# Second layer of a two-layer expert network: 64 of 256 tokens gather their rows, the V product is turned round, and VectorE divides in the mixer

## The chip, the cores and the metric

One Trainium2 chip, one of its cores. The metric is the device time in microseconds (us) from launch to end. The engines are PE (TensorE; PEld is its weight loads), DVE (VectorE), ACT (ScalarE), POOL (GpSimd, which issues part of the DMAs) and SP (SyncE, which issues DMAs alone).

## The reference, cut to what matters

256 tokens of width 1024 go through two layers (`first_block`) and a third block (`second_block`, which the change leaves alone). A layer is a mixer (attention and a convolution) and an expert part, `peer`. In layer 0 `peer` also treats 256 context tokens; in layer 1 it treats the 256 tokens alone.

```python
def peer(h, w_pq, sub_keys, u_tab, v_tab):          # h: 256 x 1024 in layer 1
    q = (h @ w_pq).reshape(B, T, PEER_HEADS, 2, PEER_HALF)
    s = jnp.einsum('bthcd,hckd->bthck', q, sub_keys)
    top_s, top_i = lax.top_k(s, PEER_TOPK)
    ...
    expert = i1 * PEER_KEYS + i2                     # 8 heads x 16 = 128 experts of 16384 per token
    w = jax.nn.softmax(best_s, axis=-1)
    ...
        u = jnp.take(u_tab, ec, axis=0)
        act = jax.nn.gelu(jnp.einsum('cd,ced->ce', hc, u), approximate=False)
        v = jnp.take(v_tab, ec, axis=0)
        return jnp.einsum('ce,ced->cd', (act * wc), v)
```

`u_tab` and `v_tab` are 16384 x 1024 in f32, 64 MB each and layer. The mixer's attention is a softmax over 512 keys, 8 heads, then times V.

## The kernel before, in words

**Two ways for a token.** The *dense* way works out gelu(U h) for all 16384 experts and multiplies by a weight that is zero for all but the token's 128. The tables pass once, in 128 tiles a of 128 rows (0.5 MB each), two tiles to a DMA of SP into a ring of four slots. The *gathered* way fetches the 128 chosen rows of U and of V of each token with indirect DMAs of POOL, one token to a partition; VectorE takes each row's product with h (`u_row`) or adds the row times its factor (`v_row`). In layer 0 the first 128 of the 512 tokens are gathered (`b.first` 128), 384 are dense (`b.D`). In layer 1 `b.first` is 0 and all 256 are dense.

**U stage** (`peer` of each engine's program). Each U tile is cut into a high and a low part of type fp32r: ACT casts the high part (`high`, L980), VectorE or POOL subtracts to get the low (`low`, L1415; POOL at L2130). PE multiplies by h in three products over 8 blocks of 128, so 24 multiplies a tile with the tile as the fixed operand and the dense tokens as the moving one (`u_product`, L757). ACT takes gelu (L1229), POOL stores the result to `g_scratch` (L2140).

**The order within it.** The U tiles are the filling between steps of choosing the experts. `early()` gives five steps to a tile, 640 in all, and `FILLS[l]` says how many steps each engine takes after each piece of work: fill_a after each of 4 groups of scores, fill_b after each of 2 groups of candidates (together the *search*, 4 fill_a + 2 fill_b), fill_c three times in the *rest*, and fill_w after each *quad* of 4 tokens whose one-hot rows are built (VectorE L1415 and L1420, ACT L1248 and L1253) and multiplied (L802) to make the weights, which ACT copies out (L1281) and POOL stores (L2170). This goes round per block t of 128 tokens. What is left of the 640 steps then runs by itself: the *tail*. In the search POOL does the low parts of even tiles, in the rest and in the quads VectorE does all. `U_TURNS` names the tiles beside which rows of U are taken; only layer 0 has them.

**V stage.** For each tile a: weigh the gelu by the weights (L1415), split it in high and low, split the V tile, and multiply (L822). The token side `x` is the fixed operand, 128 tokens at a time, the V tile the moving one, 512 columns at a time: 12 multiplies a tile in layer 1, into four PSUM banks. At the end ACT (L1298) and VectorE (L1865) copy the banks out, PE transposes (L534) and VectorE adds to `xT` (`("xp", l, m)`). Rows of V in layer 0 land in 8 buffers, by `V_TURNS`, 128 rows over 118 tiles.

**Mixer.** `attend` takes 16 units in layer 1. VectorE finds the maximum (L1527), ACT takes the exponential with its sum (L1079), VectorE the reciprocal, ACT multiplies the unit by it (L1088), two units behind; then PE transposes it. Between units VectorE does 7 taps of the convolution (L1423).

**Queues that the change touches.** POOL's is in strict order: low parts, gathers (`u_row`, `v_row`: each waits for VectorE to free its buffer), gelu stores, stores of weights, loads of both back (L2180, L2190). SP issues the ring's loads.

Of the kernel before, what the change touches and what calls it, by code (L numbers as in the profile page):

```python
# [60 lines left out]
GATHERED = 128  # L61

U_ROWS, V_ROWS = 4, 8


FILLS = ((6, 10, 14, 3), (12, 22, 20, 2))

ACT_TOKENS = (0, 1)
LAG = 3
# [6 lines left out]
def _u_turns():  # L76
    fill_a, fill_b, fill_c, fill_w = FILLS[0]
    search, rest = 4 * fill_a + 2 * fill_b, 3 * fill_c
    tiles, step = [], search + 2 * fill_c
    for t in range(1, 4):  # L80
        begin, step = step + search, step + search + rest + 32 * fill_w
        tiles += [a for a in range(128) if begin + (10 if t == 1 else 0) <= 5 * a + 3 < (step if t < 3 else 636)]
    turns = [[] for _ in range(128)]
    for i, a in enumerate(tiles):
        turns[a] = list(range(128 * i // len(tiles), 128 * (i + 1) // len(tiles)))
    return turns


U_TURNS = _u_turns()
V_TURNS = [[] for _ in range(6)] + [list(range(128 * i // 118, 128 * (i + 1) // 118)) for i in range(118)] + [[]] * 4  # L90
# [87 lines left out]
class Attention:  # L178
# [3 lines left out]
    def __init__(self, tag, q, kT, vtok, groups, lay, bias=None, sinks=None):  # L182
# [7 lines left out]

        self.score_banks, self.turn_banks, self.out_banks = ((0, 1, 2), (3,), (4, 5)) if bias is None else (
# [19 lines left out]
class Memory:  # L211


    def __init__(self, nc, ctx, A, out, book):
# [10 lines left out]
        self.u_rows = [plain[:, 14336 + 1024 * i:15360 + 1024 * i] for i in range(2)]  # L225
        self.v_rows = [plain[:, 1024 * i:1024 * i + 1024] for i in range(V_ROWS)]
# [36 lines left out]
        self.v_row_in = [signal(f"v_row{i}_in", 16) for i in range(V_ROWS)]  # L263
# [67 lines left out]
    def peer(self, l):  # L331
# [6 lines left out]
        b.first = 0 if l == 1 else GATHERED  # L338
# [3 lines left out]
        b.u_split, b.v_split = ((0, 1, 2, 3),) * 2 if l == 1 else ((0, 1, 4), (0, 1))  # L342
# [4 lines left out]
        if b.first:  # L347
            b.idx = lay.take(128).bitcast(U32)
            b.dot, b.w0 = lay.take(128), lay.take(128)
# [15 lines left out]
        if b.first:  # L365
            b.hx = lay.take(1024)
        b.qT = lay.take(8 * b.T).rearrange("p (t k q) -> p t k q", k=8, q=128)
        if b.first:

            self.u_rows += [b.qT[:, t].rearrange("p k q -> p (k q)") for t in range(2)]  # L370
# [4 lines left out]
        b.sum = lay.take(1024) if b.first else None  # L375
        return b

# [123 lines left out]
def tensor_program(e, M):  # L501
# [125 lines left out]
    def attend(a, side=lambda: None):  # L627
# [10 lines left out]
        def turned(n):  # L638
            N = a.width(n)
            P = a.P3[n % 4][:, 0:N]  # L640
            w.wait_ge(act, ("pn", a.tag, n))
# [91 lines left out]
    def peer(l):  # L733
# [7 lines left out]
        if b.first:  # L741
            for i in range(2):
                w.wait_ge(dve, ("h", ("peer", l), 4 * i + 3))
                o = bank(("hx", i), (act, ("hx", i)))
                transposes(o, [M.ACC[:, 4 * i + k, 0:128] for k in range(4)]).then_inc(pe.after(("hx", i)), 1)
# [33 lines left out]
        for t in range(T // 128):  # L779
# [10 lines left out]
            if 128 * t < b.first:  # L790
                continue
# [4 lines left out]
            for _ in range(32):  # L796
# [14 lines left out]
        for tb in range(D // 128):  # L811
            for half in range(2):
                bank(("y", l, tb, half), (act if half == 0 else dve, ("yout", l, tb, half)), (2 * tb + half,))
        for a in range(128):
            name, x = ("v", l, a), M.AG[(a + 2) % 4]
            v = M.SR[book.buffer.get(name, 0)]
            w.wait_ge(*M.low(name))
            w.wait_ge(dve, ("alow", l, a))
            for tb in range(D // 128):
                for r, c in ((0, 0), (0, 1), (1, 0)):  # L820
                    for half in range(2):
                        ins = e.matmul(M.PS[2 * tb + half][:, :], x[:, r, 128 * tb:128 * tb + 128],  # L822
                                       v[:, c, 512 * half:512 * half + 512], start=(a == 0 and (r, c) == (0, 0)),
                                       stop=(a == 127 and (r, c) == (1, 0)), skip_group_check=True)
                if a == 127:
                    ins.then_inc(pe.after(("y", l, tb), ("used", name), ("vused", l, a)), 1)
# [129 lines left out]
def scalar_program(e, M):  # L956
# [221 lines left out]
    def peer(l):  # L1178
# [26 lines left out]
        def a_high(a):  # L1205
# [5 lines left out]
            elif b.first:  # L1211
                w.wait_ge(pe, ("pu", l, 127))
# [1143 lines left out]
```

## Time and profile before

| | us |
|---|---|
| median of 3 runs | 3453.84 |
| lowest and highest | 3448.07, 3458.24 |
| the profiled execution's own time | 3468.33 |
| its span | 3466.5 |
| layer 1: mixer and projection, from L822's last to L757's first | 1652 to 1929 |
| layer 1: U stage | 1929 to 2403 |
| layer 1: V stage | 2403 to 2752 |

A row of a view by windows gives, for a stretch in us from the span's start, each engine's busy time with its number of instructions, the share of TensorE's clock that was granted, the share of the time that the 16 DMA engines were busy, and what they moved in GB/s. A row of the chain of work that ended last gives the start, the length and the instructions. A row of a group of instructions gives line, engine, operation, operands, shapes and count, then busy time and the mean of one in ns, then the idle time ahead of them and what ended it. On PE an instruction's shown length is longer than its distance to the next, since they overlap; the distance is what counts for the time. An f32 multiply shows as two records, an fp32r one as one.

### The profile page before, as it was taken

To read this page: it belongs to the slowest core of one execution; us is meant where nothing else is said; L and a number is where in the kernel's file an instruction comes from. 1 tells how busy PE (TensorE), PEld (TensorE's weight loads), DVE (VectorE), ACT (ScalarE), POOL (GpSimd) and SP (SyncE) were. 2 spreads that over 40 slices of the span, in tenths; PEclk is the share of its full clock that TensorE was granted. 3 is DMA by queue.
4 is the path that set the end of the run, shared out by engine and by line. 5 is a ranking of instruction groups with operands and counts; after the bars stand their busy time and mean duration, and the time that the engine had idled before them with its cause. 6 is when DMAs were issued, how large, how long until landed. Compare 5 with 4: busy or idle time off the path is not lost.

```text
span 3466.5 us, 48055 instructions
## 1 busy us (share of the span) xinstructions
PE 3211.1 (93%) x18889; PEld 2763.8 (80%) x18889; DVE 2353.8 (68%) x4633; ACT 1554.6 (45%) x2856; POOL 775.3 (22%) x773
## 2 busy tenths in 40 slices
PE   6997999989999999999898999999999899887898
PEld 4654799989989888888656989899888798744897
DVE  2685489897887788888584777755766655486540
ACT  2354334736556333333444476764444442223430
POOL 0000046555655444442000314221111000000000
PEclk8998999999999999999888999999999999955999
DMA  6386347968789999997366566677888554401443
GB/s 205 108 266 221 104 147 244 340 229 312 264 288 351 369 358 364 372 359 275 98 204 227 187 210 206 213 274 247 288 290 290 189 168 129 135 13 61 134 145 111
DMA packets 355697, 779.48 MB, mean 225 GB/s; under 512 B 18832, under 2 KB 237968, under 8 KB 334864
## 3 DMA queue, kind: packets, MB, share of 16 engines
q1 hardware_dynamic: 274128, 470.32, 40.0%
q0 software_dynamic: 78976, 302.04, 24.2%
q10 hardware_dynamic: 2368, 4.05, 0.3%
q8 instruction: 150, 2.46, 0.3%
q14 instruction: 75, 0.61, 0.1%
HBM read 691.39 MB, written 84.93 MB: 224 GB/s over the span
## 4 chain that ended last, share of the span: by engine, by line
PE 73%; DVE 17%; ACT 7%; DMA 2%; issue 1%; POOL 0%; DVEq 0%; SPq 0%; ACTq 0%
PE ps L822 25%; PE ps L757 16%; PE ps L529 15%; PE ps L871 4%; DVE fr L1415 3%; PE ps L593 3%; DVE area L1415 3%; PE ps L802 2%; PE ps L546 2%; PE ps L580 2%; ACT fr L980 2%; DVE area L1423 1%; DVE acc L1415 1%; ACT area L1253 1%; PE ps L558 1%; ACT area L1248 1%
## 5 line engine op out<-in xcount | busy, mean ns | idle before, releaser
L1415 DVE TENSOR_TENSOR fr<-ring,fr 128x1024 fp32r<-128x1024 f32 x623 | 775.4, 1248 | 648.9 <-ACT fr L980 647.4
L980 ACT CAST fr<-ring 128x1024 fp32r<-128x1024 f32 x678 | 707.1, 1047 | 688.1 <-PE ps L822 487.8
L757 PE MATMUL ps<-fr 128*128 128x384 f32 (+1 forms) x6144 | 964.1, 314 | 12.0 <-DVE fr L1415 12.0
L757 PEld LDWEIGHTS ps<-fr 128*128 128x128 f32 x6144 | 913.9, 192 | 18.2 <-DVE fr L1415 15.5
L822 PE MATMUL ps<-fr 128*128 128x512 f32 x3840 | 872.4, 389 | 5.0 <-DVE fr L1415 5.0
L822 PEld LDWEIGHTS ps<-fr 128*128 128x128 f32 x3840 | 721.7, 188 | 155.4 <-ACT area L1229 5.1
L529 PE MATMUL ps<-fr 128*128 128x256 f32 (+1 forms) x3312 | 485.1, 309 | 30.7 <-DVE fr L1415 30.7
L529 PEld LDWEIGHTS ps<-fr 128*128 128x128 f32 x3312 | 451.6, 196 | 63.1 <-DVE fr L1415 37.4
L2140 POOL DMA_DIRECT2D g_scratch<-area x256 | 144.2, 563 | 772.1 <-ACT area L1229 705.7
L1229 ACT ACTIVATE area<-ps 128x384 f32<-128x384 f32 (+1 forms) x256 | 113.6, 444 | 398.5 <-PE ps L757 392.4
L2130 POOL TENSOR_TENSOR fr<-ring,fr 128x1024 fp32r<-128x1024 f32 x55 | 134.5, 2445 | 451.2 <-ACT fr L980 450.7
L1415 DVE TENSOR_TENSOR area<-area 128x256 f32<-128x256 f32 (+7 forms) x365 | 196.0, 541 | 6.4 <-DMA area<-w_scratch 4.3
L2115 POOL DMA_INDIRECT plain<-in_peer_v,area x128 | 143.1, 1118 | 187.9 <-DVE area L1423 167.0
L802 PE MATMUL ps<-area 128*128 128x128 f32 x1280 | 172.5, 278 | 12.6 <-ACT area L1253 8.8
L802 PEld LDWEIGHTS ps<-area 128*128 128x128 f32 x1280 | 160.9, 191 | 22.1 <-DVE fr L1415 12.2
L1468 DVE RECIPROCAL area<-area 128x256 f32<-128x256 f32 (+1 forms) x19 | 42.9, 2258 | 190.8 <-ACT area L1009 186.9
L2190 POOL DMA_DIRECT2D area<-g_scratch x128 | 93.8, 733 | 338.0 <-DVE fr L1415 307.4
L1423 DVE SCALAR_TENSOR_TENSOR area<-plain,area 128x1024 f32<-128x1024 f32 x127 | 162.4, 1279 | 1.0
L871 PE MATMUL ps<-area,ring 128*128 128x256 f32 x704 | 157.1, 384 | 5.8 <-DMA ring<-in_w_down 4.4
L871 PEld LDWEIGHTS ps<-area,ring 128*128 128x128 f32 x704 | 135.2, 193 | 25.2 <-DMA ring<-in_w_down 4.8
L1423 DVE SCALAR_TENSOR_TENSOR area<-area,vec 128x256 f32<-128x256 f32 (+1 forms) x282 | 154.0, 608 | 0.6
L1253 ACT ACTIVATE area<-area 128x128 f32<-128x128 f32 x320 | 143.0, 508 | 0.0
(179 smaller groups left out, 3267.2 us busy)
## 6 DMA issues: line engine op xcount, KB each, us to landing
ring<-in_peer_uT SPq DMA_DIRECT2D x128, 1024.0 KB, 5.3
ring<-in_peer_v SPq DMA_DIRECT2D x128, 1024.0 KB, 8.2
ring<-in_w_mod SPq DMA_DIRECT2D x48, 1024.0 KB, 6.0
w_scratch<-acc POOLq DMA_DIRECT2D x40, 1024.0 KB, 7.2
ring<-in_w_ada SPq DMA_DIRECT2D x36, 1024.0 KB, 5.0
g_scratch<-area POOLq DMA_DIRECT2D x128, 192.0 KB, 5.4
area<-g_scratch POOLq DMA_DIRECT2D x64, 384.0 KB, 8.6
area<-w_scratch POOLq DMA_DIRECT2D x16, 1536.0 KB, 10.2
```

The lines of the kernel that those rows point to most:

```text
L529: ins = e.matmul(o, lhs, rhs, start=(n == 0), stop=(n == len(pairs) - 1))
L757: ins = e.matmul(o[:, 0:D], pairs[m][0], pairs[m][1], start=(m == 0), stop=(m == 23))
L802: ins = e.matmul(o[:, 128 * j:128 * j + 128], b.OH[:, half, 0, j, :], b.OH[:, half, 1, j, :], start=True, stop=True)
L822: ins = e.matmul(M.PS[2 * tb + half][:, :], x[:, r, 128 * tb:128 * tb + 128], v[:, c, 512 * half:512 * half + 512], start=(a == 0 and (r, ...
L871: ins = e.matmul(o[:, 0:256], piece[:, k, :], M.F[:, 11 * kh + k, :], start=(kh == 0 and k == 0), stop=(kh == 1 and k == 10))
L980: e.copy(hi, x).then_inc(act.after(("high", name)), 1)
L1253: e.activation(x, x, ACT.Relu, scale=b.iT[:, 3, tok:tok + 1], bias=b.iT[:, 2, tok:tok + 1]).then_inc(act.after(("oh", l, quad)), 1)
L1415: return e.tensor_tensor(o, a, b, op).then_inc(dve.after(*labels), 1)
L1423: return e.scalar_tensor_tensor(out=o, in0=a, scalar=s, in1=b, op0=op0, op1=op1).then_inc(dve.after(*labels), 1)
L2115: e.indirect_dma_start(M.v_rows[k % V_ROWS], None, A["peer_v0"], bass.IndirectOffsetOnAxis(ap=b.idx[:, k:k + 1], axis=0)).then_inc(M.v_row ...
L2130: e.tensor_tensor(v[:, 1, :], M.u_tile(l, c), v[:, 0, :].bitcast(F32), SU).then_inc(pool.after(("low", name)), 1)
L2140: e.dma_start(M.g_scratch[a, :, 0:D], b.GS[a % b.ngs]).then_inc(M.g_stored[a % b.ngs].after(("g", l, a)), 16)
```

## The change

- `GATHERED` is (128, 64): in layer 1 the first 64 tokens are gathered and 192 are dense. Token p's first 64 experts are fetched on partition p, its other 64 on partition p + 64, so 64 gathers of 128 rows serve them for U and 64 for V. For this two DMAs of POOL copy the second half of the indices and of the weights to partitions 64 to 127, and h of the 64 tokens is written twice before it is transposed.
- The multiplies of layer 1's U stage have 192 moving columns for 256. The quads fall from 64 to 48.
- In layer 1's V stage the split V tile is the fixed operand and the 192 tokens are the moving one: 24 multiplies of 192 columns a tile, into eight banks. The gathered sums are added by products with the two halves of the identity. The copies out and the transposes go.
- `FILLS[1]` is (14, 25, 24, 4) for (12, 22, 20, 2). V tiles of layer 1 are split in three buffers, not four; the rows of V land in six.
- In layer 1's mixer VectorE multiplies by the reciprocal, three units behind.

```diff
-GATHERED = 128
-U_ROWS, V_ROWS = 4, 8
-FILLS = ((6, 10, 14, 3), (12, 22, 20, 2))
+GATHERED = (128, 64)
+U_ROWS = 4
+FILLS = ((6, 10, 14, 3), (14, 25, 24, 4))
...
+        if t == GATHERED[l] // 128:
+            begin += 10 + (l == 1) * rest
+        tiles += [a for a in range(128) if begin <= 5 * a + 3 < (step if t < (1 if l == 1 else 3) else 636)]
...
+def _v_turns(n):
+    return [[]] * 6 + [list(range(n * i // 118, n * (i + 1) // 118)) for i in range(118)] + [[]] * 4
...
+        self.act_divides = tag != ("first", 1)
+        self.rec_lag = REC_LAG if self.act_divides else LAG
...
+        self.u_rows = [[plain[:, o:o + 1024] for o in at] for at in ((14336, 15360), (12288, 13312, 14336, 15360))]
+        self.v_rows = [[plain[:, o:o + 1024] for o in at]
+                       for at in (range(0, 8192, 1024), (0, 1024, 2048, 3072, 6144, 7168))]
...
-        b.u_split, b.v_split = ((0, 1, 2, 3),) * 2 if l == 1 else ((0, 1, 4), (0, 1))
+        b.u_split, b.v_split = ((0, 1, 2, 3), (0, 1, 2)) if l == 1 else ((0, 1, 4), (0, 1))
...
# tensor_program
+            for a in range(128):
+                ...
+                w.wait_ge(dve, ("alow", l, a))
+                if a == 127:
+                    w.wait_ge(dve, ("vrow", l, b.first - 1))
+                for m in range(8):
+                    for c, r in ((0, 0), (0, 1), (1, 0)):
+                        ins = e.matmul(M.PS[m][:, b.first:T], v[:, c, 128 * m:128 * m + 128], x[:, r, 0:D],
+                                       start=(a == 0 and (c, r) == (0, 0)), stop=(a == 127 and (c, r) == (1, 0)),
+                                       skip_group_check=True)
+                    if a == 127:
+                        for h in range(2):
+                            ins = e.matmul(M.PS[m][:, 0:64], b.sum[:, 128 * m:128 * m + 128],
+                                           M.c("ident")[:, 64 * h:64 * h + 64], start=(h == 0), stop=(h == 1))
+                        ins.then_inc(pe.after(("yt", l, m)), 1)
...
# vector_program, attend
+                if not a.act_divides:
+                    P = a.P3[m % 4][:, 0:a.width(m)]
+                    last()
+                    ts(P, P, rec, None, M_, None, ("pn", a.tag, m))
...
# vector_program, choose
+        if 128 * t < b.first:
+            tt(b.w0.rearrange("p (h r) -> p h r", r=16), ww, of_sum, M_)
+            stt(b.R1f, b.I1, 128.0, b.I2, M_, AD)
             last()
-            e.tensor_copy(b.idx, b.I1).then_inc(dve.after(("experts",)), 1)
+            e.tensor_copy(b.idx, b.R1f).then_inc(dve.after(("experts", l)), 1)
+        if 128 * (t + 1) > b.first:
+            tt(ww, ww, of_sum, M_, ("ww", l, t))
...
# vector_program, peer
+        for k in range(8):
+            n = b.first
+            if n == 64:
+                ts(M.ACC[:, k, n:128], M.ACC[:, k, 0:n], M.MOD[l][:, 24 + k, 0:1], None, AD, None)
+                last()
+            ts(M.ACC[:, k, 0:n], M.ACC[:, k, 0:n], M.MOD[l][:, 24 + k, 0:1], None, AD, None, ("h", ("peer", l), k))
...
# gpsimd_program, peer
+            if (l, t) == (1, 0):
+                w.wait_ge(dve, ("experts", l))
+                e.dma_start(b.idx[64:128, 0:64], b.idx[0:64, 64:128]).then_inc(M.moved.after(), 16)
+                e.dma_start(b.w0[64:128, 0:64], b.w0[0:64, 64:128]).then_inc(M.moved.after(("weights",)), 16)
             fill(fill_c)
+            if (l, t) == (1, 0):
+                w.wait_ge(M.moved, ("weights",))
+                for k in range(U_ROWS):
+                    u_row(k)
```

## Rows read from the trace of the kernel before

**Rows 1.** The page: span, busy times, DMA and GB/s in 40 slices.

```profile
span 3466.5 us, 48055 instructions
...
PE 3211.1 (93%) x18889; PEld 2763.8 (80%) x18889; DVE 2353.8 (68%) x4633; ACT 1554.6 (45%) x2856; POOL 775.3 (22%) x773
...
PE   6997999989999999999898999999999899887898
...
DMA  6386347968789999997366566677888554401443
GB/s 205 108 266 221 104 147 244 340 229 312 264 288 351 369 358 364 372 359 275 98 204 227 187 210 206 213 274 247 288 290 290 189 168 129 135 13 61 134 145 111
```

**Rows 2.** Windows of layer 1's U and V stages; the columns stand above.

```profile
1929.00:2036.00 107.00, 99.45 (x769) 97.69 (x770) 91.69 (x247) 49.76 (x76) 37.98 (x39) 0.94 0.59 204
1958.00:2019.00 61.00, 56.54 (x466) 55.84 (x465) 60.28 (x135) 27.84 (x41) 24.81 (x25) 1.00 0.65 223
2036.00:2108.00 72.00, 69.13 (x554) 65.15 (x553) 50.29 (x102) 71.26 (x178) 14.77 (x19) 1.00 0.67 213
2108.00:2210.00 102.00, 96.45 (x778) 94.86 (x778) 84.87 (x241) 46.29 (x74) 41.62 (x42) 0.98 0.61 210
2210.00:2282.00 72.00, 68.91 (x549) 64.79 (x550) 50.95 (x105) 71.70 (x180) 14.75 (x19) 1.00 0.68 220
2282.00:2403.00 121.00, 121.00 (x1011) 121.00 (x1010) 49.30 (x42) 53.88 (x83) 27.91 (x49) 1.00 0.73 255
2403.00:2751.00 348.00, 347.78 (x1535) 287.75 (x1534) 240.95 (x384) 172.56 (x256) 50.88 (x75) 1.00 0.79 281
```

**Rows 3.** Chain that ended last, 2280 to 2760 us: start, length, what.

```profile
2282.36 118.08 PE ps L757 x984
...
2403.52 348.61 PE ps L822 x1536
```

**Rows 4.** The same chain in layer 0's U stage.

```profile
465.61 44.93 PE ps L757 x258
```

**Rows 5.** Timeline of weight loads ahead of multiplies of one column.

```profile
1756.94 0.52 PEld L558 LDWEIGHTS ps<-con,mrow 128*128 128x128 f32 x4 [0.96 <-ACT mrow L992]
```

**Rows 6.** Timeline of weight loads in a quad.

```profile
2100.55 0.97 PEld L802 LDWEIGHTS ps<-area 128*128 128x128 f32 x8 [0.67 <-DVE fr L1415]
```

**Rows 7.** Chain in a stretch of f32 multiplies of 256 columns.

```profile
2943.17 9.50 PE ps L871 x44
```

**Rows 8.** Groups by form, whole span: VectorE's gathered rows and weighing.

```profile
L1423 DVE SCALAR_TENSOR_TENSOR area<-plain,area 128x1024 f32<-128x1024 f32 x127 | 162.4, 1279 | 1.0
...
L1786 DVE SCALAR_TENSOR_TENSOR plain<-plain,area 128x1024 f32<-128x1024 f32 x64 | 77.3, 1219 | 4.1 <-DMA plain<-in_peer_u,area 4.1
...
L1415 DVE TENSOR_TENSOR area<-area 128x384 f32<-128x384 f32 x128 | 70.6, 552 | 4.3 <-DMA area<-w_scratch 4.3
...
L1415 DVE TENSOR_TENSOR area<-area 128x256 f32<-128x256 f32 x144 | 59.9, 418 | 0.4
```

**Rows 9.** A window of layer 0's quads, and one of layer 1's attention.

```profile
595.00:701.00 106.00, 106.00 (x702) 105.86 (x702) 89.22 (x169) 85.03 (x194) 59.33 (x54) 1.00 0.97 337
1752.00:1815.00 63.00, 61.17 (x401) 30.98 (x400) 54.73 (x162) 30.60 (x70) 0.00 (x0) 0.86 0.69 225
```

**Rows 10.** The page's DMA issues: a store of 192 KB, us to landing.

```profile
g_scratch<-area POOLq DMA_DIRECT2D x128, 192.0 KB, 5.4
```

**Rows 11.** DMA issues: a gather of 128 rows of U, us to landing.

```profile
plain<-in_peer_u,area POOLq DMA_INDIRECT x64, 7.8
```

**Rows 12.** Groups in layer 1's attention: ACT's division, VectorE's reduction.

```profile
L1088 ACT ACTIVATE area<-area 128x512 f32<-128x512 f32 x16 | 11.5, 721 | 0.0
...
L1527 DVE TENSOR_REDUCE area<-ps 128x1 f32<-128x512 f32 x16 | 10.9, 681 | 0.8 <-PE ps L635 0.8
```

**Rows 13.** Timeline of PE after the V stage's last multiply.

```profile
2752.88 1.94 PE L534 MATMUL ps<-con,area 128*128 128x128 f32 x16 [0.77 <-ACT area L1298]
...
2756.61 3.72 PE L580 MATMUL ps<-acc,con 128*128 128x256 f32 x16 [1.79 <-ACT acc L1002]
```

More of the change, by code:

```diff
@@ L374, in peer, with block_of @@
         b.Y = [b.WG[0][:, 1024 * i:1024 * i + 1024] for i in range(D // 128)]
-        b.sum = lay.take(1024) if b.first else None
-        return b
+        b.sum = lay.take(1024)
+        b.u_rows, b.v_rows = self.u_rows[l], self.v_rows[l]
+        return b
+    def block_of(self, l, quad):
+        return (GATHERED[l] + 4 * quad) // 128
     def u_tile(self, l, a):
@@ L740, in peer @@
                 n_first=2)
[L741 to L745, printed above, removed]
+        for i in range(2):
+            w.wait_ge(dve, ("h", ("peer", l), 4 * i + 3))
+            o = bank(("hx", l, i), (act, ("hx", l, i)))
+            transposes(o, [M.ACC[:, 4 * i + k, 0:128] for k in range(4)]).then_inc(pe.after(("hx", l, i)), 1)
         def u_product(a, steps):
@@ L795, in peer @@
             fill(fill_c)
-            for _ in range(32):
+            for _ in range(min(128, 128 * (t + 1) - b.first) // 4):
                 half = quad % 2
@@ L809, in peer @@
         pe.note(("chosen", l))
[L811 to L818, printed above, removed]
-            for tb in range(D // 128):
[L820 to L824, printed above, removed]
-                if a == 127:
-                    ins.then_inc(pe.after(("y", l, tb), ("used", name), ("vused", l, a)), 1)
-            if a < 127:
-                ins.then_inc(pe.after(("used", name), ("vused", l, a)), 1)
@@ L1289, in peer @@
         for a in range(1, 128):
-            if b.first and a == 2:
-                w.wait_ge(dve, ("urow", 127))
-                e.activation(b.dot, b.dot, ACT.Gelu).then_inc(act.after(("dot",)), 1)
+            if a == 2:
+                w.wait_ge(dve, ("urow", l, b.first - 1))
+                e.activation(b.dot, b.dot, ACT.Gelu).then_inc(act.after(("dot", l)), 1)
             v_high(a)
             a_high(a)
-        w.wait_ge(dve, ("aw", l, 119))
-        for tb in range(D // 128):
+        if l == 0:
+            w.wait_ge(dve, ("aw", l, 119))
+        for tb in range(D // 128 if l == 0 else 0):
             w.wait_ge(pe, ("y", l, tb))
@@ L1794, in early @@
                 yield
-                for k in U_TURNS[a] if b.first else ():
+                for k in U_TURNS[l][a]:
                     u_row(k)
@@ L2208, in peer @@
             pass
-        if b.first:
-            w.wait_ge(pe, ("pu", l, 127))
-            for k in range(V_ROWS):
-                v_row(k)
+        w.wait_ge(pe, ("pu", l, 127))
+        for k in range(len(b.v_rows)):
+            v_row(k)
         for a in range(128):
```

219 lines of the change are left out of this document (121 added, 98 removed).

## The prediction, made before the change was run

> **What bounds the kernel now.** I read the page first. PE is busy 93% of the span and VectorE 68% [rows 1], so PE is the first suspect, but such shares are means over stages. So next the windows, cut at the stages of layer 1 [rows 2]. The first search with its rest (1929 to 2036) takes 107 us; in its middle, 1958 to 2019, VectorE is busy 60.28 of 61 us, so there choosing the experts sets the pace and the U tiles only fill. The second takes 102. The quads (twice 32, 72 us each) have ACT busy 71.26 of 72: 2.25 us a quad, set by ACT with PE close behind. The tail (121 us) and the whole V stage (348) have PE busy throughout. The sum of layer 1's U stage is 474 us. The chain that ended last says the same: 984 multiplies of 256 columns in 118.08 us, 120.0 ns apart, and 1536 of 512 columns in 348.61 us, 227.0 ns apart [rows 3]. Layer 0 gives 258 of 384 columns in 44.93 us, 174.1 ns [rows 4].
>
> **What one multiply of 192 columns costs.** This decides the case, and no row shows it: all fp32r multiplies here have 256 columns or more. The three distances lie on a line, 13 ns plus 0.418 ns a column (107.0 ns for 256 columns more), which gives 93 ns at 192. But each multiply also loads new weights of 128 x 128. Where multiplies have one column the loads alone set the pace: four take 0.52 us from the first's start to the last's end [rows 5], and in a quad eight take 0.97 [rows 6], so four more add 0.45, 112 ns each. I take 112, the nearest in kind, since 93 lies under what a load needs. Lower bound 93; 120 if fp32r's 13 ns come on top of a load too; and, far off, the pace of plain f32, whose 256 columns take two records of 216 ns (44 in 9.50 us [rows 7]), 1.69 ns a column, 324 ns at 192. The Trainium skill ("TensorE: Matmul & The Clock Gate", section "LDWEIGHTS") says that a load takes its columns over 1.2 GHz, however few rows it has; that is 107 ns for 128 columns, speaks against narrowing below 256, and the loads above agree.
>
> A tile is then 24 x 0.112 = 2.69 us, in the U stage for 2.88, in the V stage for 12 x 0.227 = 2.72. Narrowing the dense side by a quarter gains 7% there and turning V round 1% here, because the number of loads doubles.
>
> **U stage, by its new steps.** Search and rest now take 2 x (106 + 72) steps, 71.2 tiles; 48 quads 38.4 tiles; the tail 18.4 (before: 60.8, 25.6, 41.6).
> - *First search and rest.* VectorE sets it. It gets 25.0 low parts for 21.2, at 1.17 us (49.30 us for the tail's 42 instructions [rows 2]), +4.4; index, weights and a copy ahead of the transposes +0.6. 107 + 5 = 112 us. PE needs 35.6 x 2.69 + 4 = 100, so it waits.
> - *Second.* The same 4.4, and rows of U from tile 69 on, 64 rows over 69 tiles: 8.9 rows in the part of the rest where VectorE is the bound, at 1.22 us [rows 8]: +10.9. 102 + 15 = 117.
> - *Quads.* PE: 8 records of 0.112 and 0.8 tile of 2.69, 3.05 us. VectorE had 50.29 / 32 = 1.57 with 0.4 low part, now 1.10 + 0.8 x (1.17 + 0.93 x 1.22) = 2.94; ACT 2.23 with 0.4 tile at 1.30 (53.88 us for the tail's 41.6), now 2.75. Bytes: 0.8 x (0.524 for U, 0.098 stored, 0.93 x 0.524 gathered) and 0.262 of weights stored = 1.15 MB; at the 337 GB/s of layer 0's quads [rows 9], 3.41 us, of which the ring's four slots and the slack of the search cover a part. I take 3.2: 48 x 3.2 = 154 us.
> - *Tail.* 18.4 x 2.69 = 49, +4 since 1.11 MB a tile asks for over 400 GB/s where the best slice has 372 [rows 1]: 53.
>
> 112 + 117 + 154 + 53 = 436 for 474: **-38 us**.
>
> **V stage.** VectorE had 240.95 us, 1.88 a tile [rows 2]. 64 fewer columns save it 0.13 twice over two operations (552 against 418 ns for 128 columns [rows 8], a half of that each), and 64 rows over 118 tiles add 0.54 x 1.28: 2.44 us, under PE's 2.69. Bytes a tile: 0.524 + 2 x 0.098 + 0.54 x 0.524 = 1.005 MB; at 372 GB/s 2.70 us, so DMA and PE are level and DMA slightly behind. 118 x 2.70 + 10 x 2.69 = 345, +2 for a ring that the U tail left empty: 347 for 349: **-2**. A gather lands in 7.8 us where a store of 192 KB takes 5.4 [rows 10, 11]; six buffers at a row each 5 us hide it.
>
> **Small terms.** Before the U stage VectorE writes h in 16 short operations; it does so while PE still projects, and what is left with PE's 8 transposes and their copies costs +1 (0 if hidden, 4 if VectorE's low parts come late). POOL copies indices and weights by two DMAs, waits, then issues four gathers, behind gelu stores that go at PE's pace. The first row is wanted 10 steps (2.5 quads, 8 us) after that; landing alone takes 7.8 [rows 11]. What waits behind the row on VectorE are one-hots, and PE behind these: +4, from 0 to 11. Mixer: ACT loses 16 divisions of 0.72 us where it is busy 30.60 of 63 us [rows 9, 12]; VectorE gets them, at a guess 0.5 to 0.68 each (the latter its reduction over the same 512 [rows 12]), and has 54.73 of 63 us, some 15 units, so it rises to about 62: level with PE's 61. +1, from -2 to +6. End of the V stage: the copies and transposes between the last multiply and the sum of squares go (2752 to 2756.6 [rows 13]), but the last tile is longer by 32 records of 0.11 us: -1.
>
> **Sum:** -38 - 2 + 1 + 4 + 1 - 1, and +2 for handing over between stages that are now all nearly level: **-33 us**. The profiled execution took 3468.33, 14.5 above the median; its time would be 3435, the median 3453.8 - 33 = **3421**.
>
> **Rivals.**
> 1. *The load costs fp32r's 13 ns too, 120 ns.* For it: every fp32r distance seen has them. Against: where loads bind, 112. The U stage becomes 112 + 118 + 158 + 53 = 441 (-33), V 128 x 24 x 0.120 = 369 (+20), the small terms +7: -6, 3448.
> 2. *The DMA engines are the bound.* For it: demand is 1.15 MB a quad and 1.0 a tile, and layer 0 had 97% DMA busy at 337 GB/s [rows 9]. At 348 GB/s in V and 337 in U: V 118 x 2.89 + 27 = 368 (+19), quads 164, tail 61, U 454 (-20), the small terms +7: +6, 3460. Against: the slices of 351 to 372 GB/s in layer 0's V stage, with PE at 9 tenths or more in each [rows 1]. The Trainium skill ("DMA: Bandwidth & Descriptors", "Specifications") has about 358 GB/s as the limit of a core's HBM side; by it V would be 358, 11 more than my sum. The highest slices, 369 and 372 GB/s, lie above it.
> 3. *Slower: the narrow form falls to plain f32's pace.* One mechanism, in both stages: 256 tiles x 24 x 0.324 = 1991 us, with quads and scores 2050 for the present 823: +1227, 4680. It decides from where a multiply passes about 119 ns: -33 is used up by 4435 multiplies (all of V, and the U tiles of quads and tail) at 7.4 ns more. For it: nothing but that fp32r below 256 columns is unseen. Against: the three distances have no step.
> 4. *The load hides after all, 93 ns.* Then DMA holds V at 345 and VectorE the quads at 2.94: about -41, 3413. Against: rows 5 and 6. The Trainium skill (same page as above, "Back-to-back issue gap") gives 81 ns at 128 columns and 131 at 512 for a stream of pairs, 89 at 192 between them; at 512 the trace has 227, so I don't lean on it.
> 5. *The change doesn't do what it says* in one part: the division moved to VectorE, and the turned V, bring nothing. That is in my sum.
>
> **Chances.** My forecast with its spread 0.55, rival 1 0.14, rival 2 0.12, rival 3 0.08, rival 4 0.07, gathers or fills going wrong in a way I haven't listed 0.04. A measurement of this kernel can tell about 0.3%, 10 us. Faster by more: 0.51 of my case, all of rival 4, a third of rivals 1 and 2: 0.66. Same: most of the rest of these: 0.18. Slower: rival 3, the unlisted, part of rival 2: 0.16. The range leaves out rival 3 and the unlisted: from 3390 (93 ns, no DMA limit, small terms at their low ends) to 3466 (rival 2 with small terms high).
>
> **What would show it.** Right: multiplies of 192 columns 112 ns apart in the tail; V stage near 347 us with PE busy throughout or short waits on DMA; U stage near 436, the second search longer than before. Wrong: a distance of 93, 120 or over 300; VectorE waiting for gathers for tens of us; DMA share at 0.97 with idle PE.

## The result, and the profile after

The changed kernel takes 3420.41 us (median of 4 runs, 3416.32 to 3425.84), the kernel before 3452.80 us in the same comparison (median of 4). The ratio is 0.989, with a 95% interval of 0.9874 to 0.9907: 32 us less, where 33 less had been forecast (3421). The profiled execution's own time is 3416.32 us, its span 3414.5.

The page of the changed kernel, its first lines, as in [rows 1]:

```profile
span 3414.5 us, 51179 instructions
...
PE 3153.6 (92%) x20321; PEld 2776.8 (81%) x20321; DVE 2463.3 (72%) x4809; ACT 1511.8 (44%) x2761; POOL 1008.0 (30%) x901
...
PE   6997999998999999999898999899999899877898
...
PEclk9998999999999999999989999999999999956999
DMA  6386346968879999998357577899999654401443
GB/s 216 107 288 200 105 146 236 334 237 302 284 269 345 381 360 367 361 365 325 105 166 235 197 256 273 281 371 374 375 373 384 209 173 125 140 1 62 136 149 110
```

PE is busy less (3153.6 us for 3211.1) though its trace has 1432 more records of multiplies; the DMA engines move more, and slices 28 to 31, the end of the tail and most of the V stage, stand at 373 to 384 GB/s, where slices 29 to 31 had 288 to 290 before. PEclk is the granted clock in tenths of full speed.

The windows of layer 1, columns as in [rows 2]: first search and rest, 16 quads, second search and rest, 32 quads, tail, V stage, and the V stage's middle.

```profile
1922.00:2028.00 106.00, 103.11 (x893) 101.95 (x893) 92.48 (x252) 54.13 (x85) 46.52 (x48) 0.98 0.65 226
2028.00:2076.00 48.00, 47.09 (x414) 46.62 (x415) 41.99 (x78) 42.98 (x100) 28.64 (x29) 1.00 0.96 348
2076.00:2198.00 122.00, 106.68 (x910) 104.28 (x908) 107.56 (x274) 50.92 (x84) 75.36 (x64) 0.96 0.74 259
2198.00:2299.00 101.00, 99.44 (x859) 98.45 (x860) 90.84 (x165) 88.35 (x206) 55.69 (x54) 0.98 0.95 348
2299.00:2357.00 58.00, 51.82 (x457) 51.17 (x456) 40.72 (x55) 24.17 (x41) 36.63 (x41) 0.99 0.99 388
2357.00:2700.00 343.00, 343.00 (x3049) 343.00 (x3049) 293.93 (x445) 172.11 (x256) 179.91 (x138) 0.99 0.96 360
2400.00:2680.00 280.00, 280.00 (x2510) 280.00 (x2510) 246.74 (x371) 141.99 (x209) 157.32 (x118) 1.00 0.99 373
```

The first search and the V stage are PE's. In the second search VectorE is busy 107.56 of 122 us. The quads and the tail have the DMA engines at 0.95 to 0.99.

The chain of work that ended last, in which [rows 3] had 984 and 1536 multiplies:

```profile
2319.59 14.85 DMA plain<-in_peer_u,area
...
2344.65 9.03 DMA g_scratch<-area
...
2356.70 343.75 PE ps L867 x3051
2706.33 3.52 PE ps L599 x16
```

The V stage is one run of 3051 multiplies in 343.75 us: 112.7 ns each. Ahead of it the chain goes through POOL's gathers, their landing, and stores of gelu: the tail is no longer PE's.

Stage by stage, from the start of each stage's first multiply to the start of the next one's (V to its own last multiply). Code that is the same in both kernels, layer 0, took 1636.9 to 1652.7 us in the fourteen traces of this case, and the mixer of layer 1 270 to 281: so much a single trace scatters there, and the spans are not compared, only stages.

| us | before | predicted change | after | after, a second trace |
|---|---|---|---|---|
| first search and rest | 104.5 | +5 | 103.6 | 105.0 |
| quads (64, then 48) | 144.6 | +10 | 148.3 | 148.3 |
| second search and rest | 101.8 | +15 | 122.0 | 122.3 |
| tail | 121.4 | -68 | 58.1 | 59.8 |
| U stage | 472.3 | -38 | 432.0 | 435.4 |
| V stage | 348.2 | -2 | 349.4 | 348.1 |
| V's last multiply to the third block's first weights | 23.3 | -1 | 18.5 | 18.5 |

The second trace is of the same kernel, run again beside the experiments:

> The changed kernel once more, as the yardstick of this set. Expected 3417 to 3424 us, ratio to before 0.989 to 0.992; layer 1's U stage 430 to 436 us, its V stage 349 us.

Measured: 3416.28 us (4 runs), ratio 0.9904 with 0.9874 to 0.9935.

### The profile page after: what moved, and what is told of

It is laid out like the page before. It is cut to its first block, busy times and chain, and to the rows that moved or that the text cites. A ratio compares the mean times of both kernels' runs of the same rounds, so it can differ in the third digit from the quotient of the medians.

```text
span 3414.5 us, 51179 instructions
## 1 busy us (share of the span) xinstructions
PE 3153.6 (92%) x20321; PEld 2776.8 (81%) x20321; DVE 2463.3 (72%) x4809; ACT 1511.8 (44%) x2761; POOL 1008.0 (30%) x901
## 4 chain that ended last, share of the span: by engine, by line
PE 72%; DVE 20%; ACT 4%; DMA 2%; issue 1%; POOL 0%; DVEq 0%; SPq 0%; ACTq 0%; POOLq 0%
PE ps L841 15%; PE ps L775 15%; PE ps L548 15%; PE ps L867 10%; PE ps L911 4%; DVE fr L1458 3%; DVE area L1458 3%; PE ps L820 3%; PE ps L612 3%; DVE area L1466 2%; PE ps L599 2%; PE ps L565 2%; DVE acc L1458 1%; ACT fr L1020 1%; DVE plain L1838 1%
## 5 line engine op out<-in xcount | busy, mean ns | idle before, releaser
L775 PE MATMUL ps<-fr 128*128 128x384 f32 (+1 forms) x6144 | 935.6, 310 | 20.9 <-DVE fr L1458 20.9
L775 PEld LDWEIGHTS ps<-fr 128*128 128x128 f32 x6144 | 889.2, 192 | 28.2 <-DVE fr L1458 25.5
L841 PE MATMUL ps<-fr 128*128 128x512 f32 x2304 | 523.9, 390 | 3.2 <-DVE fr L1458 3.2
L841 PEld LDWEIGHTS ps<-fr 128*128 128x128 f32 x2304 | 433.4, 188 | 93.5 <-ACT area L1268 3.5
L548 PEld LDWEIGHTS ps<-fr 128*128 128x128 f32 x3312 | 449.2, 195 | 62.9 <-DVE fr L1458 37.4
L867 PE MATMUL ps<-fr 128*128 128x192 f32 x3072 | 347.7, 275 | 3.5 <-DVE fr L1458 3.5
L867 PEld LDWEIGHTS ps<-fr 128*128 128x128 f32 x3072 | 346.5, 193 | 3.6 <-ACT fr L1020 3.6
L2172 POOL DMA_INDIRECT plain<-in_peer_v,area x192 | 270.7, 1410 | 257.3 <-DVE area L1466 166.8
L1466 DVE SCALAR_TENSOR_TENSOR area<-plain,area 128x1024 f32<-128x1024 f32 x190 | 243.0, 1279 | 1.0
L2165 POOL DMA_INDIRECT plain<-in_peer_u,area x128 | 199.8, 1561 | 89.2 <-DVE plain L1838 63.5
L1458 DVE TENSOR_TENSOR area<-area 128x384 f32<-128x384 f32 (+8 forms) x367 | 190.2, 522 | 5.7 <-DMA area<-w_scratch 3.6
L1838 DVE SCALAR_TENSOR_TENSOR plain<-plain,area 128x1024 f32<-128x1024 f32 x128 | 155.4, 1219 | 18.3 <-DMA plain<-in_peer_u,area 18.3
L820 PE MATMUL ps<-area 128*128 128x128 f32 x1152 | 154.8, 277 | 7.6 <-ACT area L1292 3.5
```

Source lines behind the costliest of these rows:

```text
L548: ins = e.matmul(o, lhs, rhs, start=(n == 0), stop=(n == len(pairs) - 1))
L775: ins = e.matmul(o[:, 0:D], pairs[m][0], pairs[m][1], start=(m == 0), stop=(m == 23))
L820: ins = e.matmul(o[:, 128 * j:128 * j + 128], b.OH[:, half, 0, j, :], b.OH[:, half, 1, j, :], start=True, stop=True)
L867: ins = e.matmul(M.PS[m][:, b.first:T], v[:, c, 128 * m:128 * m + 128], x[:, r, 0:D], start=(a == 0 and (c, r) == (0, 0)), stop=(a == 127 ...
L1458: return e.tensor_tensor(o, a, b, op).then_inc(dve.after(*labels), 1)
L1466: return e.scalar_tensor_tensor(out=o, in0=a, scalar=s, in1=b, op0=op0, op1=op1).then_inc(dve.after(*labels), 1)
```

## What a multiply of 192 columns costs

The distance from one multiply's start to the next one's, in the loop of the V stage, worked out from the start times in each trace (median; in brackets the mean without the pauses over 400 ns):

| moving columns, fp32r | stage and trace | distance, ns | granted clock of the stage |
|---|---|---|---|
| 512 | V, before | 227 (227) | 1.00 |
| 256 | V, counts alone with V turned | 120 (120.5) | 1.00 |
| 224 | V, 32 tokens gathered | 113 (112.6) | 0.99 |
| 192 | V, after | 111 (112.8) | 0.99 |
| 160 | V, narrowed further | 213 | 0.50 |
| 128 | V, narrowed further | 213 (213.4) | 0.50 |

At full clock this is the forecast's line down to 256 columns and then its floor of 112. The last two rows come from kernels that leave tokens out of the multiplies (the last 64, the last 32), and no step of the forecast had them. The edit, with 128; that with 160 is the same:

```diff
# 192 columns in the U and the V stage of layer 1 become 128
+            n_c = 128 if l == 1 else D
-            pairs = M.three(..., lambda s, k: HR[:, s, k, b.first:T], range(8))
+            pairs = M.three(..., lambda s, k: HR[:, s, k, b.first:b.first + n_c], range(8))
-                    ins = e.matmul(o[:, 0:D], ...
+                    ins = e.matmul(o[:, 0:n_c], ...
-                        ins = e.matmul(M.PS[m][:, b.first:T], v[...], x[:, r, 0:D],
+                        ins = e.matmul(M.PS[m][:, b.first:b.first + 128], v[...], x[:, r, 0:128],
```

> The changed kernel, but the multiplies of layer 1's U and V stages take 128 moving columns; the last 64 tokens are left out of them. Theory of the load: distance 109 to 112 ns as at 192, U stage and V stage unchanged within 3 us. Theory of a time per column: 13 + 0.418 x 128 = 67 ns at least somewhere, the V stage then down to what DMA gives, about 330 us.

Measured: 3842.84 us (one run), 420 more than the changed kernel. The page's granted clock in 40 slices, and windows of the first search, the first quads, the second search with its rest (to 2237 us, then on to 2293), two parts of the tail, and the V stage:

```profile
PEclk8998999999999999988955969655555569975899
```

```profile
1923.00:2112.00 189.00, 189.00 (x885) 187.97 (x885) 90.28 (x253) 52.33 (x85) 45.78 (x48) 0.50 0.37 128
2112.00:2161.00 49.00, 48.29 (x414) 47.86 (x414) 40.78 (x75) 41.91 (x97) 26.86 (x28) 0.97 0.92 327
2165.00:2237.00 72.00, 70.56 (x621) 69.70 (x621) 64.25 (x221) 34.29 (x53) 43.82 (x37) 1.00 0.65 218
2238.00:2293.00 55.00, 53.40 (x250) 53.04 (x249) 42.99 (x57) 14.89 (x27) 28.38 (x25) 0.50 0.81 280
2397.00:2425.00 28.00, 26.34 (x236) 26.20 (x235) 16.97 (x22) 10.26 (x17) 19.12 (x22) 1.00 1.00 391
2426.00:2471.00 45.00, 44.98 (x211) 44.79 (x210) 23.20 (x32) 12.31 (x21) 15.69 (x17) 0.50 0.64 243
2472.00:3133.00 661.00, 661.00 (x3100) 661.00 (x3100) 303.17 (x452) 168.48 (x264) 116.57 (x139) 0.50 0.54 188
```

PE is busy all 661 us of the V stage, and the granted clock there is 0.50, the 1.2 GHz level of the two; in the quads between, whose U multiplies have the same 128 columns, it is 0.97. The first search takes 189 us for 104, and the tail 75.1 for 58.1, because the clock falls halfway in it, behind 28 us at 1.00 with PE busy 26.34 of them.

The fall at the start of the U stage is not this kernel's own. The kernel before, with 256 columns, has it too, and is back at 1.00 after it:

```profile
1930.00:1936.00 6.00, 5.03 (x24) 4.76 (x23) 5.90 (x20) 3.98 (x4) 0.00 (x0) 0.50 0.83 306
```

With 128 columns the clock stays at 0.50 for the whole first search. But 128 columns and a busy PE do not always bring the fall: from 2165 to 2237 us the same loop of U multiplies has 1.00, with PE busy 70.56 of 72 us. What decides between the two is open.

The chain says what a whole stage at 0.50 costs:

```profile
2471.40 651.14 PE ps L868 x3051
```

213.4 ns a multiply for 112.7, in the same count: the distance goes with the granted clock. In the short stretches at 0.50 of the kernel before, U multiplies of 256 columns are 213 ns apart too (median of 61). Where the clock stayed up in the kernel with 128, its U multiplies are 109 to 114 ns apart (median 111), no nearer than those of 192: that is the floor, seen at a width where 13 + 0.418 x 128 would give 67. The Trainium skill ("TensorE: Matmul & The Clock Gate", "LDWEIGHTS") has a load take its columns over 1.2 GHz, 107 ns here. At full granted clock the traces agree (109 to 113); at 0.50 they do not (213).

How near is 192 columns to that? 160 in their place:

> The changed kernel, but the multiplies of layer 1's U and V stages take 160 moving columns; the last 32 tokens are left out of them. With 128 columns the granted clock stood at 0.50 in the first search and the whole V stage, and the distance at 213 ns. [...] Theory 2 (192 is near the edge): clock 0.50 in part or all of the V stage, 500 to 660 us.

Measured: 3849.20 us (one run). First search and V stage:

```profile
1925.00:2115.00 190.00, 189.54 (x882) 188.44 (x882) 90.23 (x252) 52.19 (x84) 45.11 (x48) 0.50 0.37 129
2480.00:3140.00 660.00, 660.00 (x3086) 659.19 (x3086) 300.52 (x453) 166.28 (x260) 111.77 (x135) 0.50 0.54 186
```

The clock stands at 0.50 in the same two stages, and in part of the second search and of the tail, as with 128 columns (132.0 and 72.8 us long). Whether the V multiplies of 160 columns would keep 112 ns at full clock is not seen, since it was never granted there. In the V stage 192 columns have 0.99 in the changed kernel; widths between 160 and 192 were not run.

## Which part of the change brings what

**The counts alone.** The kernel before with one line changed: all 256 tokens dense.

```diff
-FILLS = ((6, 10, 14, 3), (12, 22, 20, 2))
+FILLS = ((6, 10, 14, 3), (14, 25, 24, 4))
```

> The kernel before with FILLS[1] = (14, 25, 24, 4) and nothing else: no gathered tokens in layer 1, 64 quads, 256 moving columns. Theory A (the fill counts bring the U stage's gain, since PE stood idle for some 40 us of 474 while VectorE and ACT set the pace of search and quads): searches 107 + 4 and 102 + 4, 64 quads at 0.9 + 0.8 x 2.88 = 3.2 us = 205, tail 5.6 tiles = 16 and a few us of waits for the weights' loads: 439 for 474, total 3418 to 3430. Rival B (the gathering of 64 tokens brings it: fewer quads, fewer columns): fills alone bring under 10 us, 3445 or more.

Measured: 3433.90 us (10 runs), ratio 0.9938 with 0.9919 to 0.9957; U stage 445.0, V stage 349.7. First search, quads, second search, quads, tail:

```profile
1920.00:2030.00 110.00, 109.65 (x885) 108.68 (x885) 89.31 (x247) 53.34 (x82) 44.08 (x45) 0.98 0.66 224
2030.00:2131.00 101.00, 100.48 (x845) 99.29 (x846) 64.41 (x119) 90.19 (x206) 21.80 (x32) 1.00 0.72 237
2131.00:2243.00 112.00, 111.45 (x919) 110.13 (x917) 90.31 (x246) 53.04 (x83) 47.58 (x48) 1.00 0.67 223
2243.00:2344.00 101.00, 100.83 (x848) 99.56 (x848) 64.47 (x118) 89.83 (x205) 21.75 (x32) 1.00 0.71 234
2344.00:2365.00 21.00, 18.70 (x156) 18.52 (x156) 6.48 (x9) 8.25 (x14) 8.98 (x14) 1.00 0.90 332
```

PE is busy 109.65 of 110, 100.48 of 101, 111.45 of 112 and 100.83 of 101 us. The kernel before left PE idle in the searches (99.45 busy of 107 [rows 2]); the new counts move the tiles from the tail (20.6 us for 121.4) into those gaps, and into quads that ACT had bound. That is 27 of the U stage's 37 to 40 us, from one line. In these rows PE's idle time falls from 19 us of 474 to 4 of 445; the other 12 us lie in multiplies that stand closer (124.3 ns of busy time a record before, 120.8 here). The expectation's "some 40 us" of idle time is more than the rows show.

**Gathering without narrowing.** The changed kernel, its U multiplies with all 256 columns again.

```diff
# tensor_program, U stage, l == 1: c0 = 0 for b.first
-            ... HR[:, s, k, b.first:T] ...  o[:, 0:D]
+            ... HR[:, s, k, c0:T] ...       o[:, 0:T - c0]
# gelu reads columns 64 to 255 of it
```

> The changed kernel, but the U stage's multiplies of layer 1 take all 256 columns again (the 64 gathered tokens' columns are computed and not used). Spacing 120 ns for 112. My theory (PE sets only the quads and the tail, and in the tail DMA is level): 38.4 tiles x 24 x 8 ns = +7 us, total 3425 to 3430. Rival (narrowing pays in every multiply): 3072 x 8 ns = +25 us, 3443 to 3448.

Measured: 3431.12 us (6 runs), ratio 0.994 with 0.992 to 0.996; U stage 444.0. First and second search, tail:

```profile
1926.00:2035.00 109.00, 108.45 (x884) 107.48 (x883) 89.85 (x251) 51.23 (x83) 46.34 (x48) 0.98 0.63 216
2085.00:2210.00 125.00, 112.61 (x903) 109.96 (x901) 108.52 (x273) 50.41 (x82) 73.83 (x64) 0.97 0.72 248
2312.00:2369.00 57.00, 55.66 (x461) 55.14 (x459) 40.59 (x53) 23.75 (x40) 34.96 (x40) 1.00 1.01 398
```

Against the counts alone, 16 quads go (51.4 us), but the 12.8 tiles in them come back in the tail (+37, 2.88 us each), and the rows of U cost 15 in the second search: 444 for 445, nothing. What gathering makes possible is the narrowing, from 444 to 432 or 435 us. In the first search, where no row is gathered, it gives 109.5 - 103.6 = 5.9 (35.6 tiles x 24 x 7.5 ns would be 6.4; by the second trace 4.5); in the second 4.2; in the tail nothing, 57.3 against 58.1 and 59.8, though PE needs 4 us less there: 398 GB/s and a share of 1.01 stand in its way already at 256 columns.

**V round and not.** The changed kernel with the V tile as the moving operand again, for its 192 dense tokens, with the copies out and the transposes.

```diff
-                for m in range(8):
-                    for c, r in ((0, 0), (0, 1), (1, 0)):
-                        e.matmul(M.PS[m][:, b.first:T], v[:, c, 128 * m:128 * m + 128], x[:, r, 0:D], ...
+                for tb, t0, nt in ((0, 0, 128), (1, 128, 64)):
+                    for r, c in ((0, 0), (0, 1), (1, 0)):
+                        for half in range(2):
+                            e.matmul(M.PS[2 * tb + half][0:nt, :], x[:, r, t0:t0 + nt],
+                                     v[:, c, 512 * half:512 * half + 512], ...
```

> The changed kernel, but layer 1's V tiles are the moving operand again (12 multiplies of 512 columns a tile, the second six with 64 tokens fixed), with copies out and transposes at the end. My theory (turning V round changes the pace of a tile from 2.72 to 2.71 us): V stage 349 us, then 4 to 6 us of copies and transposes come back and the last tile gets 3 us shorter: 3420 to 3427. Rival (turning is what paid for the gathered rows): +10 us or more.

Measured: 3428.71 us (10 runs), ratio 0.9925 with 0.9904 to 0.9946. The median is 12 us above that of the changed kernel run beside it, though the two intervals overlap, so the stages have to say it. The chain:

```profile
2349.95 352.59 PE ps L868 x1536
```

The stage takes 352.2 us for 348.1 to 349.4, and from its last multiply to the third block 26.8 us for 18.5: together 11 to 12 us, 8 of them the end and 3 to 4 the stage. As the moving operand V costs 12 multiplies of 512 columns whether the tokens are 192 or 256; gathering 64 tokens saves nothing there unless V is turned.

**V turned for 256 tokens.** The kernel with the new counts alone, and its V tile fixed: 24 multiplies of 256 columns.

```diff
-    (as before: x fixed, 12 multiplies of 512 columns, copies, transposes)
+    e.matmul(M.PS[m][:, 0:T], v[:, c, 128 * m:128 * m + 128], x[:, r, 0:D], ...   # 24 of 256 columns
```

> The kernel before with the changed fill counts and layer 1's V tiles as the fixed operand, no token gathered: 24 multiplies of 256 columns a tile. Theory (13 ns + a column's time above some 230 columns, the load below): 120 ns, V stage 369 us, 20 more than the form of before; the way to the next stage 19 us for 23. Rival (turning pays by itself): V stage 350 us or less.

Measured: 3441.99 us (one run), V stage 370.1 for 349.7. Its chain:

```profile
2359.65 367.84 PE ps L850 x3051
```

120.6 ns each. So turning costs 20 us in the stage at 256 columns and gains 3 to 4 at 192; the way from the stage's end to the next one falls from 23.3 to 20.5 us here, and is 18.5 in the changed kernel.

**The division.** `self.act_divides = True`, in the changed kernel.

> The changed kernel, but ACT divides in layer 1's mixer, two units behind. My theory (VectorE and PE are level there): the attention of layer 1 takes the same 83 us within 2, total within 3 us of the changed kernel's. Rival (the move pays): the attention 4 us or more longer with ACT. Second rival (it costs, VectorE being the bound): 3 us or more shorter with ACT.

Measured: 3415.34 us (4 runs), ratio to before 0.9872 with 0.9854 to 0.9891: no difference. A window of the attention in the changed kernel, then in this one:

```profile
1744.00:1807.00 63.00, 61.23 (x400) 30.86 (x399) 58.37 (x168) 23.21 (x57) 0.00 (x0) 0.86 0.69 223
```

```profile
1732.00:1795.00 63.00, 61.84 (x428) 31.86 (x426) 55.72 (x165) 30.77 (x70) 0.00 (x0) 0.89 0.76 245
```

PE is busy 61.2 and 61.8 of 63 us in both, so ACT's 7.6 us less and VectorE's 2.7 more make no difference to it. VectorE's division took 487 ns a unit:

```profile
L1462 DVE TENSOR_SCALAR area<-area 128x512 f32<-128x512 f32 x16 | 7.8, 487 | 0.6
```

## What bounds the V stage and the tail

**V: PE or the DMA engines.** Only 8 of the 64 rows of V are gathered.

```diff
-V_TURNS = [_v_turns(n) for n in GATHERED]
+V_TURNS = [_v_turns(128), (rows 0 to 7 beside tiles 6 to 13, then none)]
```

> The changed kernel with 8 of the 64 gathers of V rows and their additions in layer 1; 56 are left out, some 29 MB. Theory of the load: V stage within 2 us of 349, since PE sets it although DMA showed 99% busy at 373 GB/s; DMA busy share then 0.8. Rival (DMA or VectorE is the bound): the V stage falls by 5 us or more and the distance from 112.8 to 110 ns or less.

Measured: 3423.11 us (one run). The middle of the V stage, and its chain:

```profile
2410.00:2680.00 270.00, 270.00 (x2420) 270.00 (x2419) 178.05 (x303) 130.67 (x203) 42.20 (x63) 1.00 0.78 269
```

```profile
2363.34 343.63 PE ps L869 x3051
```

269 GB/s and a DMA share of 0.78, for 373 and 0.99; VectorE 178.05 of 270 us; and 3051 multiplies in 343.63 us for 343.75. Neither the transfers nor VectorE hold it. PE does, at a distance that at full clock is the same for 128, 160 and 192 columns (U stages, medians 111 to 112 ns): that of the loads.

**The rows of U.** Half of them, in the changed kernel (`U_LEFT = (128, 32)` in place of 64, where the turns are laid out and waited for).

> The changed kernel with 32 of its 64 gathers of U rows and their products in layer 1; the other 32 are left out. Theory (in the tail the DMA engines are the bound, in the second search VectorE is, rows weighing on both): second search 122 to 115 us, tail 59 to 51, the quads as before; U stage 417 to 422 for 434. Rival (rows hide): U stage 430 or more.

Measured: 3408.00 us (one run); U stage 420.1. Second search, tail:

```profile
2077.00:2193.00 116.00, 105.89 (x907) 103.74 (x905) 99.37 (x262) 51.23 (x84) 62.12 (x57) 0.97 0.71 238
2293.00:2344.00 51.00, 50.75 (x455) 50.59 (x453) 30.67 (x38) 22.89 (x39) 22.41 (x31) 1.00 0.93 341
```

32 rows fewer: the second search 116.2 for 122.0 to 122.3, the tail 51.6 for 58.1 to 59.8, with PE busy 50.75 of 51 there. So what the tail has above PE's need is due to the rows. The V stage takes 352.5 us, 3 more than in the changed kernel, since its first load of gelu back lands later, after 13.0 us; the whole gains 8 to 12 us. The waits of the changed kernel's tail and second search (who waited for what: us in total, times, longest):

```profile
ACT area L1268 <- DMA g_scratch<-area: 25.4, 10, 4.7
...
DVE plain L1838 <- DMA plain<-in_peer_u,area: 12.0, 8, 3.2
```

```profile
PE ps L553 <- DVE area L1458: 6.9, 1, 6.9
```

In the tail ACT waits 25.4 us for stores of gelu to leave its buffers, which share POOL's queue with the gathers, and VectorE 12.0 us for rows. Whether the order of the queue or the full DMA engines (0.99, and 0.93 with half the rows) delays them, no run separates. In the second search PE waits 6.9 us once, for VectorE's last step of the choice (L553), and VectorE works off 15 rows of U there. Around and behind that wait the granted clock is 0.50 for 10 us:

```profile
L1838 DVE SCALAR_TENSOR_TENSOR plain<-plain,area 128x1024 f32<-128x1024 f32 x15 | 18.3, 1218 | 0.0
```

```profile
2175.00:2185.00 10.00, 3.71 (x18) 3.72 (x19) 9.55 (x15) 1.17 (x3) 6.28 (x5) 0.50 0.89 305
```

**32 tokens on four partitions each.** 224 are dense; h written four times, six small DMAs for indices and weights, four pieces of the identity.

```diff
-GATHERED = (128, 64)
+GATHERED = (128, 32)
```

> The changed kernel with 32 gathered tokens in layer 1 for 64, each token's 128 rows on four partitions: 32 gathers for U, 32 for V, 224 moving columns, 56 quads. Theory (a weight load of 109 to 112 ns sets a multiply's pace at 224 columns as at 192, so a gathered row less costs PE nothing but its share of the quads): distance 110 to 113 ns; the second search gets 5 us shorter, 8 quads more add 24 us, the tail loses 6.4 tiles and its waits for DMA, -24; U stage 425 to 431 for 434, V stage 348 to 351, total 4 to 9 us under the changed kernel's. Rival (the columns count, 13 ns + 0.418 ns each): 107 ns at 224 against 93 at 192, which the measured 112 at 192 already contradicts; or, with what is left of it, 117 to 120 ns at 224: U stage 440, V 365, total 15 to 25 us over the changed kernel's.

Measured: 3422.02 us (4 runs), ratio 0.9889 with 0.9871 to 0.9906: the same as the changed kernel. The U stage is shorter (428.0: second search 113.7, tail 40.4, but eight quads more), the V stage longer (356.5). In its chain:

```profile
2350.63 13.20 DMA area<-g_scratch
2365.83 321.77 PE ps L867 x2859
```

The multiplies of 224 columns cost no more in the long run (321.77 us / 2859 = 112.5 ns); the start does: the weights of the first tiles wait 13.2 us for a load of gelu back. What the tail no longer spends, V's start does.

**POOL helps in the rest too.** A try at the second search: POOL takes the low parts of even tiles also in the first two thirds of the rest, and ACT divides.

```diff
             fill(4 * fill_a + 2 * fill_b)
-            mine[0] = False
+            mine[0] = l == 1
             ...
             fill(2 * fill_c)
+            mine[0] = False
```

> An attempt at a version that beats both: the changed kernel, ACT divides in layer 1's mixer, and POOL does the low parts of even U tiles also in the first two thirds of layer 1's rests, where VectorE is the bound. Theory (VectorE sets the second search, PE idle 15 of 121 us there): second search 122 to about 117 us, first unchanged at 104 since PE is nearly full, U stage 427 to 431. Rival (POOL, 74 of 121 us busy with gathers and stores, becomes the late one): second search 122 us or more.

Measured: 3425.67 us (4 runs), ratio 0.9905 with 0.9884 to 0.9926. First search 110.6 us, second 127.5: 5 to 7 us more each. The first:

```profile
1922.00:2030.00 108.00, 102.57 (x862) 101.43 (x861) 93.01 (x242) 50.10 (x77) 58.92 (x51) 0.95 0.62 216
```

POOL is busy 58.92 us for 46.52, and VectorE not less (93.01 for 92.48), though five of its low parts went to POOL. PE is busy 102.57 of 108 us, less densely than in the changed kernel (103.11 of 106). The groups of VectorE in the first search tell why, two of the changed kernel, then the same two of this one:

```profile
L1458 DVE TENSOR_TENSOR area<-area 128x1024 f32<-128x1024 f32 x6 | 9.5, 1581 | 0.2
L1458 DVE TENSOR_TENSOR area<-area,con 128x1024 f32<-128x1024 f32 x4 | 4.9, 1225 | 0.1
```

```profile
L1458 DVE TENSOR_TENSOR area<-area 128x1024 f32<-128x1024 f32 x6 | 13.6, 2272 | 0.2
L1458 DVE TENSOR_TENSOR area<-area,con 128x1024 f32<-128x1024 f32 x4 | 8.0, 2011 | 0.1
```

The same operations take longer, 1225 ns alone and 2011 to 2272 on average here. In the U stage of nine traces, 70 such operations of VectorE start while POOL subtracts a low part, and all 70 end 1.08 to 1.09 us after POOL's has ended: they wait for it, and show as busy meanwhile, up to 3.42 us. So a low part given to POOL frees VectorE of 1.22 us, and can hold it up by as much as 2.2. Other waits may add to this; no run takes it away. No version here beats the changed kernel by more than the runs can tell.

## Why the prediction was right, step by step

- **The distance.** 112 ns, from loads in quads: 112.7 in the chain. Rivals 1 (120), 3 (324) and 4 (93) fall. This term decided between the forecast and these rivals, and it was right for the reason given.
- **First search.** "VectorE sets it", 112 us: failed. 103.6 to 105.0. I had taken the middle 61 us, in which VectorE is full, for the whole: over the stage it had 15 idle us (91.69 of 107 [rows 2]). With the counts alone PE is busy 109.65 of 110, and narrower multiplies then shorten the stage to 103.6. PE set it, at "35.6 x 2.69 + 4 = 100", 4 short.
- **Second search.** 117 predicted, 122. The direction and the reason hold (rows of U on VectorE, shown by half the rows: 116), the size was 5 short. I counted 8.9 rows there at 10.9 us, and 15 fall into it at 18.3; I did not count either that PE would wait 6.9 us for the end of the choice.
- **Quads.** 3.2 us predicted, 3.00 and 3.14 measured (47.9 / 16, 100.4 / 32), with the DMA engines at 0.95 to 0.96; 148 for 154. 348 GB/s came where I had allowed 337.
- **Tail.** 53 predicted, 58 to 60. The DMA engines gave 388 GB/s, more than the 372 I took as their best, but moved 22.5 MB where 18.4 tiles at 1.11 MB are 20.4; gelu's stores and the rows came late (25.4 and 12.0 us of waits), by the queue's order or by full engines.
- **First gather.** +4 predicted, nothing to be seen. The first gather was issued at 2026.95 us and its row used at 2037.19, with no wait for it: one-hots and low parts fill the 10 us between, and VectorE's two waits there, 2.24 and 1.23 us, are for ACT.
- **U stage.** 436 predicted, 432.0 and 435.4: four errors of 5 to 8 us that cancel, so that the sum came out this near is luck. The forecast summed stages and never asked what each part brings; the runs give the counts 27, the narrowing 9 to 12, the gathering itself none.
- **V stage.** 347 predicted, 348.1 to 349.4, for a wrong reason in part: "DMA slightly behind" fails. Taking 56 of 64 gathers away changes nothing; the 2.69 us of the loads are the bound. Rival 2 falls in the V stage, and may hold in part in the tail. The limit in the Trainium skill ("DMA: Bandwidth & Descriptors", "Specifications", about 358 GB/s) would by my estimate have made V 358; the trace disagrees, with 373 over 280 us.
- **End of V.** -1 predicted, of which the last tile's 32 records of 0.11 us stand in the V stage of the table above (its 349.4 holds 3.5 of them), and the rest shows as 23.3 to 18.5. V and its end together: -3 predicted, -3.6 and -4.9 measured. In the timeline the sums of squares (L599) begin 0.4 us behind the start of the last product, where before 4.5 us lay between the end of the multiplies and them (1536 multiplies ended at 2752.1, L580 began at 2756.6 [rows 3, 13]):

```profile
2705.76 0.57 PE L873 MATMUL ps<-con,area 128*128 128x64 f32 x4
2706.17 3.67 PE L599 MATMUL ps<-acc,con 128*128 128x256 f32 x16
```

- **Mixer.** +1, from -2 to +6: no difference, 487 ns a division where I guessed 500 to 680. The part of rival 5 about the division holds: it brings nothing. The part about V's turn does not: without it 11 to 12 us are lost, by the stages.
- **Handing over.** +2 was a guess; it stands in the stages' figures and was not measured alone.
- **What was missing.** No rival had the granted clock. At 160 columns the kernel takes 430 us more than at 192, the worst outcome near the one chosen, and my slower rival (a form that runs at plain f32's pace) stood for nothing real.

## What to carry to other kernels

At full granted clock a matmul with 128x128 of new weights each time costs the larger of its load (112 ns) and its columns; with fp32r the two meet near 237 columns (13 ns + 0.418 a column reaches 112 there; 224 measured 113), so narrowing below that is worth the difference to the meeting point and no more, and turning an operand round is free only down there. Before moving work to other engines, lay the filling work out anew: one line of counts gave about two thirds of the U stage's gain, by moving it from a stage where PE was the bound into stages where PE idled. Before giving VectorE's work to POOL, look whether the one waits for the other. And read the granted clock of each narrow loop: a PE that was never idle did not keep it up here.

## What had not been expected of the hardware

- The granted clock stood at 0.50 through loops in which PE is 100% busy, with fp32r multiplies of 128 or 160 moving columns and a new load each (213 ns apart, first search and V stage, both kernels); with 192 it was 0.95 to 0.98 in the first search, 0.94 to 1.00 in the tail and 0.99 in the V stage, over the traces. In the quads of the kernels with 128 and 160, where such multiplies stand between others, it was 0.95 to 0.97, and for 72 us of the second search with 128 it was 1.00.
- The distance follows the granted clock: 109 to 114 ns at full, 213 at half, and at half 256 columns had 213 as well.
- VectorE's operations on two operands of 128x1024 wait while POOL subtracts one of the same size: 1.22 us alone, 1.3 to 3.4 us where they began beside it, each ending 1.08 to 1.09 us behind POOL's (70 of 70 in nine traces).
- The DMA engines moved 388 GB/s in the changed kernel's tail and 398 in the one with 256 columns in its U stage, with shares of 0.99 and 1.01; the best slice before was 372.
